# Compressing keys and values inside the projections of a two-block transformer kernel

## The reference, cut to what matters

```python
def compress(kv, pos_emb, w1, w2):
    n_c = (S - CMP_LEN) // CMP_STRIDE + 1                     # 31 blocks of 32 tokens, 16 apart
    blocks = kv[:, blk] + pos_emb[None, None, :, None, :]
    flat = blocks.transpose(0, 1, 3, 2, 4).reshape(B, n_c, G, CMP_LEN * Dh)
    return jax.nn.gelu(flat @ w1) @ w2                        # 2048 -> 128 -> 64
...
k_cmp = compress(kc, pos_k, ck_w1, ck_w2)
v_cmp = compress(vc, pos_v, cv_w1, cv_w2)
s_c = einsum(qc, k_cmp) * scale          # q without rotation
s_s = einsum(qr, k_sel) * scale          # rotated q, rotated keys ks
s_w = einsum(qr, kw_i) * scale           # rotated q, rotated keys kw
```

## Time and profile before

| | before |
|---|---|
| runs (us) | 3473.38, 3473.66, 3468.51; median 3473.38 |
| profiled execution | 3475.57; its span in the trace 3473.8 |
| TensorE busy, share of the span | 3272.7 us, 94% |
| DVE, ACT, POOL busy | 46%, 41%, 46% |
| mean granted TensorE clock | 0.966 |

### The profile page before, as it was taken

How to read it: one execution, slowest core, us unless ns; L and a number is a source line. 1 busy time by engine, 2 the same in 40 slices (tenths; PEclk the granted TensorE clock), 3 DMA queues, 4 the chain that set the end, 5 groups by cost and what they waited for, 6 DMA issues and landing times.

```text
span 3473.8 us, 45512 instructions
## 1 busy us (share of the span) xinstructions
PE 3272.7 (94%) x16902; PEld 2669.8 (77%) x16902; DVE 1596.8 (46%) x2361; ACT 1438.5 (41%) x2575; POOL 1597.1 (46%) x1404
## 2 busy tenths in 40 slices
PE   6789999998999999999988996999999999999998
PEld 4567888876568888788877775888888888888886
DVE  4783443142743431444247875555565562234421
ACT  3355333223764333333235554454454532243332
POOL 4245445652555446444553321444444434464454
PEclk8899999997999999999999997999999999999999
DMA  4111333341013333333332120111111113333332
GB/s 121 45 43 55 97 97 95 94 116 37 1 32 96 96 95 95 91 97 95 96 82 60 51 61 25 31 38 42 38 37 37 41 46 99 98 95 97 97 96 68
DMA packets 471306, 245.86 MB, mean 71 GB/s; under 512 B 13819, under 2 KB 468710, under 8 KB 471014
## 3 DMA queue, kind: packets, MB, share of 16 engines
q1 hardware_dynamic: 470144, 241.33, 24.5%
q10 hardware_dynamic: 998, 2.30, 0.2%
HBM read 241.51 MB, written 2.10 MB: 70 GB/s over the span
## 4 chain that ended last, share of the span: by engine, by line
PE 84%; DVE 9%; ACT 4%; issue 2%; POOL 1%; DMA 0%; ACTq 0%; DVEq 0%; POOLq 0%
PE ps L464 18%; PE ps L466 18%; PE ps L465 18%; PE ps L2207 2%; PE ps L2311 2%; PE ps L2208 2%; PE ps L2209 2%; PE ps L1538 2%; PE ps L2293 2%; PE ps L1548 2%; PE ps L1561 1%; PE ps L1726 1%; PE ps L1799 1%; PE ps L1727 1%; PE ps L1728 1%
## 5 line engine op out<-in xcount | busy, mean ns | idle before, releaser
L446 POOL TENSOR_TENSOR w_lo<-ring,w_hi 128x512 fp32r<-128x512 f32 (+1 forms) x908 | 1222.7, 1368 | 1542.9 <-ACT w_hi L437 1542.9
L437 ACT ACTIVATE w_hi<-ring 128x512 fp32r<-128x512 f32 (+1 forms) x908 | 516.0, 617 | 1269.4 <-PE ps L466 1189.5
L464 PE MATMUL ps<-h_hi,w_hi 128*128 128x512 f32 x1776 | 702.7, 396 | 4.6 <-POOL w_lo L446 4.4
L466 PE MATMUL ps<-h_hi,w_lo 128*128 128x512 f32 x1776 | 693.4, 390 | 0.0
L465 PE MATMUL ps<-h_lo,w_hi 128*128 128x512 f32 x1640 | 640.1, 390 | 0.0
L464 PEld LDWEIGHTS ps<-h_hi,w_hi 128*128 128x128 f32 x1776 | 334.4, 188 | 81.1 <-POOL w_lo L446 6.4
L466 PEld LDWEIGHTS ps<-h_hi,w_lo 128*128 128x128 f32 x1776 | 334.1, 188 | 69.8
L465 PEld LDWEIGHTS ps<-h_lo,w_hi 128*128 128x128 f32 x1640 | 308.8, 188 | 68.2 <-issue 4.8
L465 PE MATMUL ps<-a_lo,w_hi 128*128 128x512 f32 x752 | 292.9, 390 | 0.0
L466 PE MATMUL ps<-a_hi,w_lo 128*128 128x512 f32 x720 | 280.4, 390 | 0.0
L464 PE MATMUL ps<-a_hi,w_hi 128*128 128x512 f32 x720 | 280.4, 389 | 0.0
(11 more groups left out here) (446 smaller groups left out, 5809.7 us busy)
## 6 DMA issues: line engine op xcount, KB each, us to landing
ring<-in_ffn_w_in SPq DMA_DIRECT2D x176, 512.0 KB, 3.8
ring<-in_w_in SPq DMA_DIRECT2D x96, 512.0 KB, 4.0
ring<-in_ffn_w_down SPq DMA_DIRECT2D x32, 512.0 KB, 4.1
ring<-in_ffn_w_out SPq DMA_DIRECT2D x32, 512.0 KB, 3.8
ring<-in_w_o SPq DMA_DIRECT2D x16, 512.0 KB, 4.1
ring<-in_w_branch_gdn SPq DMA_DIRECT2D x16, 512.0 KB, 3.8
ring<-in_nsa_w_in SPq DMA_DIRECT2D x15, 512.0 KB, 3.9
ring<-in_dsa_w_in SPq DMA_DIRECT2D x13, 512.0 KB, 4.1
```

What stands on the lines that cost most here:

```text
L437: act.activation(w_hi[:, (halves(u) + j) % PIECES, 0:n, :], slot(u)[:, j * n:(j + 1) * n, :], ACT.Copy) \
L446: pool.tensor_tensor(w_lo[:, q % PIECES, 0:n, :], slot(u)[:, j * n:(j + 1) * n, :], w_hi[:, q % PIECES, 0:n, :].bitcast(f32), ALU.subtract ...
L464: pe.matmul(dst, wh, hi(k), start=first and k == 0, stop=False)
L466: ins = pe.matmul(dst, wl, hi(k), start=False, stop=last and k == 2 * n - 1)
```

## The change

1. The compression moves into the loop over the projection entries. PE transposes the positions after n=9, ACT copies them at n=10; DVE gathers the blocks of keys at n=12 and of values at n=13; PE makes the first product of keys after n=15 and of values after n=16; ACT takes both GELUs at n=17; PE makes the second products after n=17 and ACT copies them at n=18, ahead of the copy of that entry itself.
2. Both groups stand side by side in one product: 16 products with 62 moving columns for each of keys and values, 32 in all, in place of 64 with 31.
3. The duplicating products (L1388, L1402) go. At n=10 ACT issues four transfers inside SBUF, each of 64 partitions x 4 KB, that write `kv_raw` and `k_rot` with the partition halves exchanged (`kv_swap`, `k_swap`). DVE gathers from `kv_raw` or `kv_swap` in SBUF, where it read PSUM.
4. `k_pad`, its 8 copies and its zeroing go: the scores read `k_rot` or `k_swap` directly, and only one copy of `k_cmp` is written. The factor 1/8 goes into the rotated queries: L1240 and L1242 become scalar_tensor_tensor, with a scale of 1 for the keys and 1/8 for the queries.
5. `pe_attention` waits for the last rotations and copies, `k_swapped` and `nsa_copied` 2.

```diff
-    blk = Area(area.at).take(2, CMP_LEN // 2, NC)
+    blk = [Area(at).take(CMP_LEN // 2, 2 * NC) for at in (area.at, prT_at)]
...
-    k_pad = area.take(2, 2, 2, T)
+    area.take(KT, T)
     gelu_h = area.take(2, 2, 32)
+    swap_area = Area(MEM_AT)
+    kv_swap, k_swap = swap_area.take(2, T), swap_area.take(2, T)
...
-    def pool_key_zeros(pool):
-
-        pool.wait_ge(unit_done.sem, p1["units"][-1] + 1)
-        for b in range(2):
-            pool.memset(k_pad[:, b], 0.0).then_inc(sig("pads_zero").sem, 1)
...
+            if n == N_POS:
+                pe_cmp_positions(pe)
+            elif n in N_HIDDEN:
+                pe_cmp_hidden(pe, N_HIDDEN.index(n))
+            elif n == N_SECOND:
+                pe_cmp_second(pe)
...
+            if n == N_POS + 1:
+                act_cmp_positions(act)
+                act_swap(act, p)
+            elif n == N_SECOND:
+                act_cmp_gelu(act)
+            elif n == N_SECOND + 1:
+                act_cmp_second(act)
...
-            dve.tensor_tensor(e[4], e[3], const("rope_c"), ALU.mult)
+            scale = HD ** -0.5 if done >= 2 else 1.0
+            dve.scalar_tensor_tensor(e[4], e[3], scale, const("rope_c"), ALU.mult, ALU.mult)
             dve.wait_ge(sig("proj_perm").sem, p["perm"] + r + 1)
-            ch.link(dve.tensor_tensor(rt[:, :], ps[:, 4 + r % 2, :], const("rope_s"), ALU.mult))
+            ch.link(dve.scalar_tensor_tensor(rt[:, :], ps[:, 4 + r % 2, :], scale, const("rope_s"), ALU.mult, ALU.mult))
...
+            if n in N_BLOCKS:
+                dve_cmp_blocks(dve, N_BLOCKS.index(n))
...
-    def pe_nsa(pe):
-        pe.wait_ge(sig("proj_rope").sem, p1["rope"] + sum(e[0] == "rope" for e in p1["entries"]))
-        pe.wait_ge(*evac_of(p1, len(p1["entries"]) - 1 - 2 * MEM_PAIRS))
-        pe.wait_ge(*evac_of(p1, len(p1["entries"]) - 1))
-        pe.wait_ge(sig("proj_turned").sem, 3)
-        for b in range(2):
-            for g in range(2):
-                ins = pe.matmul(ps[:, 2 * b + g, :], const(f"dup{g}"), k_rot[:, b, :], start=True, stop=True)
-                ins.then_inc(sig("nsa_dup").sem, 1)
+    N_POS, N_BLOCKS, N_HIDDEN, N_SECOND = MEM_FROM + KT - 1, (12, 13), (15, 16), 17
+
+    def pe_cmp_positions(pe):
         pe.wait_ge(sig("cmp_loaded").sem, 16 * 7)
         for j in range(2):
-            ins = pe.transpose(ps[:, 4, j * CMP_LEN:(j + 1) * CMP_LEN], pos_rows[0:CMP_LEN, j, :],
+            ins = pe.transpose(ps[:, 6, j * CMP_LEN:(j + 1) * CMP_LEN], pos_rows[0:CMP_LEN, j, :],
                                ident[0:CMP_LEN, 0:CMP_LEN])
         ins.then_inc(sig("pos_turned").sem, 1)
+
+    def act_cmp_positions(act):
+        act.wait_ge(sig("pos_turned").sem, 1)
+        act.activation(posT.rearrange("p j l -> p (j l)"), ps[:, 6, 0:2 * CMP_LEN], ACT.Copy).then_inc(sig("pos_ready").sem, 1)
+
+    def act_swap(act, p):
+
+        act.wait_ge(sig("mem_tile").sem, p["mem"] + KT)
+        act.wait_ge(sig("proj_evac").sem, p["evac"] + 3)
+        for e in range(2):
+            act.dma_start(kv_swap[even_odd[e]], kv_raw[even_odd[1 - e]]).then_inc(sig("kv_swapped").sem, 16)
+        act.wait_ge(sig("proj_rope").sem, p["rope"] + 2)
+        for e in range(2):
+            act.dma_start(k_swap[even_odd[e]], k_rot[even_odd[1 - e]]).then_inc(sig("k_swapped").sem, 16)
+
+    def dve_cmp_blocks(dve, j):
+        dve.wait_ge(sig("pos_ready").sem, 1)
+        dve.wait_ge(sig("kv_swapped").sem, 32)
+        dve.wait_ge(sig("proj_turned").sem, 3)
+        for g in range(2):
+            for half in range(2):
+
+                rows_ = even_odd[half]
+                kv = (kv_raw if g == half else kv_swap)[rows_, j, :]
+                src = bass.AP(kv.tensor, kv.offset + half, [kv.ap[0], [2, CMP_LEN // 2], [CMP_STRIDE, NC]])
+                pos = posT[rows_, j, half::2].unsqueeze(2).broadcast_to([HD, CMP_LEN // 2, NC])
+                ins = dve.tensor_tensor(blk[j][rows_, :, g * NC:(g + 1) * NC], src, pos, ALU.add)
+        ins.then_inc(sig("cmp_blocks").sem, 1)
+
+    def pe_cmp_hidden(pe, j):
         pe.wait_ge(sig("w1_loaded").sem, 32)
-        pe.wait_ge(sig("nsa_copied").sem, 4)
+        pe.wait_ge(sig("cmp_blocks").sem, j + 1)
+        for l in range(CMP_LEN // 2):
+            ins = pe.matmul(ps[:, 6 + j, 0:2 * NC], w1[:, j, l, :], blk[j][:, l, :],
+                            start=l == 0, stop=l == CMP_LEN // 2 - 1)
+        ins.then_inc(sig("cmp_hidden").sem, 1)
+
+    def act_cmp_gelu(act):
         for j in range(2):
-
-            if j:
-                pe.wait_ge(sig("cmp_blocks").sem, 2)
-            for g in range(2):
-                ins = pe.matmul(ps[:, 5 + g, :], const(f"dup{g}"), kv_raw[:, j, :], start=True, stop=True)
-                ins.then_inc(sig("cmp_dup").sem, 1)
-            for g in range(2):
-                pe.wait_ge(sig("cmp_blocks").sem, 2 * j + g + 1)
-                for l in range(CMP_LEN // 2):
-                    ins = pe.matmul(ps[:, 2 * j + g, 0:NC], w1[:, j, l, :], blk[:, g, l, :],
-                                    start=l == 0, stop=l == CMP_LEN // 2 - 1)
-                ins.then_inc(sig("cmp_hidden").sem, 1)
-        pe.wait_ge(sig("cmp_gelu").sem, 4)
+            act.wait_ge(sig("cmp_hidden").sem, j + 1)
+            act.activation(gelu_h[:, j, :, 0:NC], ps[:, 6 + j, 0:2 * NC].rearrange("p (g c) -> p g c", g=2),
+                           ACT.Gelu_apprx_tanh).then_inc(sig("cmp_gelu").sem, 1)
+
+    def pe_cmp_second(pe):
+        pe.wait_ge(sig("cmp_gelu").sem, 2)
         for g in range(2):
-            pe.matmul(ps[:, 7, g * 32:g * 32 + NC], w2_k, gelu_h[:, 0, g, 0:NC], start=True, stop=True)
-            ins = pe.matmul(ps[0:NC, 7, 64 + g * HD:64 + (g + 1) * HD], gelu_h[:, 1, g, 0:NC], w2_v, start=True, stop=True)
+            pe.matmul(ps[:, 6, g * 32:g * 32 + NC], w2_k, gelu_h[:, 0, g, 0:NC], start=True, stop=True)
+        for g in range(2):
+            ins = pe.matmul(ps[0:NC, 7, g * HD:(g + 1) * HD], gelu_h[:, 1, g, 0:NC], w2_v, start=True, stop=True)
         ins.then_inc(sig("cmp_done").sem, 1)
 
-    def act_nsa(act):
-        for b in range(2):
-            for g in range(2):
-                act.wait_ge(sig("nsa_dup").sem, 2 * b + g + 1)
-                act.wait_ge(sig("pads_zero").sem, 3 + b)
-                for e in even_odd:
-                    ins = act.activation(k_pad[e, b, g, even_odd.index(e), :], ps[e, 2 * b + g, :], ACT.Copy,
-                                         scale=HD ** -0.5)
-                ins.then_inc(sig("nsa_copied").sem, 1)
-        act.wait_ge(sig("pos_turned").sem, 1)
-        act.activation(posT.rearrange("p j l -> p (j l)"), ps[:, 4, 0:2 * CMP_LEN], ACT.Copy).then_inc(sig("pos_ready").sem, 1)
-        for j in range(2):
-            for g in range(2):
-                act.wait_ge(sig("cmp_hidden").sem, 2 * j + g + 1)
-                act.activation(gelu_h[:, j, g, 0:NC], ps[:, 2 * j + g, 0:NC], ACT.Gelu_apprx_tanh) \
-                   .then_inc(sig("cmp_gelu").sem, 1)
+    def act_cmp_second(act):
         act.wait_ge(sig("cmp_done").sem, 1)
-        for g in range(2):
-            for e in even_odd:
-                ins = act.activation(k_cmp[e, g, even_odd.index(e), 0:NC], ps[e, 7, g * 32:g * 32 + NC], ACT.Copy,
-                                     scale=HD ** -0.5)
-            ins.then_inc(sig("nsa_copied").sem, 1)
+        act.wait_ge(sig("pads_zero").sem, 2)
+        act.activation(k_cmp[:, :, 0, 0:NC], ps[:, 6, 0:64].rearrange("p (g c) -> p g c", g=2)[:, :, 0:NC], ACT.Copy,
+                       scale=HD ** -0.5).then_inc(sig("nsa_copied").sem, 1)
         act.activation(v_cmp[0:NC].rearrange("p (x n) -> p x n", x=5)[:, 1::2, :],
-                       ps[0:NC, 7, 64:64 + 2 * HD].rearrange("p (g d) -> p g d", g=2), ACT.Copy) \
+                       ps[0:NC, 7, 0:2 * HD].rearrange("p (g d) -> p g d", g=2), ACT.Copy) \
            .then_inc(sig("nsa_copied").sem, 1)
-
-    def dve_nsa(dve):
-        dve.wait_ge(sig("pos_ready").sem, 1)
-        for j in range(2):
-            for g in range(2):
-                dve.wait_ge(sig("cmp_dup").sem, 2 * j + g + 1)
-                if j:
-                    dve.wait_ge(sig("cmp_hidden").sem, g + 1)
-                for half in range(2):
-
-                    rows_ = slice(half * HD, (half + 1) * HD)
-                    kv = ps[rows_, 5 + g, :]
-                    src = bass.AP(kv.tensor, kv.offset + half, [kv.ap[0], [2, CMP_LEN // 2], [CMP_STRIDE, NC]])
-                    pos = posT[rows_, j, half::2].unsqueeze(2).broadcast_to([HD, CMP_LEN // 2, NC])
-                    ins = dve.tensor_tensor(blk[rows_, g], src, pos, ALU.add)
-                ins.then_inc(sig("cmp_blocks").sem, 1)
...
-                        u |= dict(q=q_raw[:, pair, tok], k=k_cmp[:, g, hh, 0:NC], bias=cmp_bias[:, t, 0:NC], masked=0,
+                        u |= dict(q=q_raw[:, pair, tok], k=k_cmp[:, g, 0, 0:NC], bias=cmp_bias[:, t, 0:NC], masked=0,
```

(11 more changed lines are left out.)

4 lines of the change are left out of this document (removed).

## The result

| | before | after |
|---|---|---|
| median of 5 runs each (us) | 3473.66 (3468.51 to 3478.0) | 3452.10 (3447.49 to 3455.53) |
| ratio to before | 1 | 0.9938, 95% interval 0.9923 to 0.9952 |
| profiled execution; its span | 3475.57; 3473.8 | 3452.10; 3450.0 |
| mean granted TensorE clock | 0.966 | 0.967 |

The kernel is faster by 21.6 us. The forecast was 29.3 us, or 3444.1; the measured median stands 0.1 us above the top of the range. The sign came out, and so did most of the mechanism; a part of the gain is missing: 7.7 us by the medians, 5.5 us by the spans of the traces (3473.8 and 3450.0).

A forecast was written before the change was run, and what follows sets the result against it. TensorE was taken to bound the kernel, with a serial 41.9 us stage before attention. The terms -41.9 + 2.3 + 6.6 + 0.3 + 3.1 + 1.0 - 0.7 sum to -29.3 us, so 3444.1 us, range 3437 to 3452.

The forecast's parts named there:

- (a): Stage between last projection product and first score goes, -41.9 us; attention's remaining wait for ACT's roundings and copies, +2.3 us.
- (f): Short memk entries before n=17 no longer outrun ACT and POOL, as other products give them time: -0.7 us.
- (b): First products, halved, in PE's own queue: 64 records at 0.103 us, +6.6 us; upper bound 13.4 at 0.209 each.
- (c): Small transposes on PE: +0.3 us; ACT's copy of them at n=10 lies beside PE's next entry.
- (d): GELU at n=17 stands behind ACT's rounding, so PE idles for roundings, table load and GELUs: +3.1 us.
- rival 3: Longer stall at n=17 or n=15, from table-switch drain or gathers blocking with POOL: +1.4 to +4 us, about 3447; chance 0.12.
- (g): DVE's rotations and block gathers, 2.7 to 4.3 us of gathers per entry, finish before PE asks: cost 0.
- (h): ACT's four transfers at n=10, 3.6 us to issue at most, cost nothing; PE is held only from 21 us on.
- Rival 4: Swaps inside SBUF land slowly: costs from 21 us landing time, kernel slower than before from 50 us; chance 0.03.
- (e): Second products, four matmuls of the compression: +1.0 us at full clock (0.8 to 1.9).
- Rival 2: Cold compression: PE drops to half clock inside the moved products, +6.8, +0.9 and +1.7 us, 3453.5 us; chance 0.08.
- rival 1: Warm attention: clock stays at 1.00 over both waits, so attention starts at full clock: 2.8 us less, 3441.3; chance 0.2.

The follow-up runs named there:

- e4: Kernel after, with first and second products, GELU and copies moved behind the last projection entry, gathers and transfers left in place; 3449.24 us, ratio 0.9937.
- e1: Kernel after, but at n=17 ACT takes both GELUs before it rounds unit n+2; 3441.36 us, ratio 0.9908 to the kernel before.
- e2: Kernel after, plus three throwaway products of 512 columns on PE ahead of its wait for GELU at n=17; 3446.41 us, ratio 0.9916.
- e6: Kernel after, idle at n=17 left, plus four throwaway products of 512 columns (eight records) behind the second products; 3457.44 us, ratio 0.9950.
- e5: e1, plus at n=18 ACT copies k_cmp and v_cmp, loads the exponential's table, and copies the entry before rounding; 3444.36 us, ratio 0.9911.
- e9: e5, plus one throwaway product of 512 columns in each of steps 1 to 5 of layer 1's attention; 3437.55 us, ratio 0.9897.
- e3: Kernel after, plus a dummy GELU behind ACT's copy at n=16 that loads the table early; 3444.03 us, ratio 0.9918.
- e8: Kernel before with only the rotated keys' part changed (k_swap, scaled queries, no k_pad), compression left behind the projections; 3469.69 us, ratio 0.9986.
- e7: Kernel after, but first products made per group again, 64 of 31 columns in place of 32 of 62; 3469.54 us, ratio 0.9984.

## Where the prediction was right, and where it failed

**What bounds the kernel: right.** The gain is in the stage: 24.0 us of the stage, 23.8 of the span, with the small differences outside it that are named above.

**(a), (f): right.** The stage is gone, and so is the wait for POOL. What attention waits for is 1.97 us, forecast 2.3, since ACT's two copies are short (0.20 and 0.25 us) and overlap. ScalarE of the kernel after, in order of time:

```profile
816.81 1.15 ACT L439 ACTIVATE w_hi<-ring 128x512 fp32r<-128x512 f32 x2 [11.93 <-PE ps L483]
817.86 0.20 ACT L1455 ACTIVATE square_sum<-ps 128x62 f32<-128x62 f32 x1
817.96 0.25 ACT L1457 ACTIVATE square_sum<-ps 31x128 f32<-31x128 f32 x1
818.12 0.36 ACT L1228 ACTIVATE arena<-ps 128x256 f32<-128x256 f32 x1
```

**(b): right, 7.0 for 6.6 us.** With 62 columns a record still costs about a weight load. The upper bound of 0.209 was real: e4's records took 0.216 at half clock. The Trainium skill (TensorE: Matmul & The Clock Gate, LDWEIGHTS) gives a weight load as its columns divided by 1.2 in ns, 107 ns for 128 columns, and names no clock; the row at full clock agrees (0.110), that of e4 at half clock disagrees, and the measurement decides.

**(c): right**, 0.30 us. **(d): right as an idle**, 2.94 for 3.1 us. ScalarE of the kernel after:

```profile
802.97 1.28 ACT L1441 ACT_TABLE_LOAD   x1
804.26 0.34 ACT L1441 ACTIVATE arena<-ps 128x62 f32<-128x62 f32 x2
```

The roundings end at 802.95, the table load runs from 802.97 to 804.25, and the GELUs start at 804.26. The Trainium skill (ScalarE: Activation LUTs, What ACT_TABLE_LOAD costs) gives a switch a drain of some 1.38 us more; this trace shows 0.02 and 0.01 us around the load, so here it isn't there, and the longer stall of rival 3 falls.

**(g): right in cost, wrong in size.** VectorE of the kernel after, in order of time:

```profile
773.86 2.03 DVE L1427 TENSOR_TENSOR arena<-squares,square_sum 64x496 f32<-64x496 f32 x1
775.90 2.03 DVE L1427 TENSOR_TENSOR arena<-arena,square_sum 64x496 f32<-64x496 f32 x2
...
785.37 1.90 DVE L1427 TENSOR_TENSOR arena<-squares,square_sum 64x496 f32<-64x496 f32 x1
```

The gathers of an entry took 5.1 and 5.0 us, where I had 2.7 to 4.3. Six of the eight took 1.0 us each; two, which began while POOL was in the middle of a split instruction, took 2.03 and 1.90. They were done at 778.97 and 787.27, and PE asked at 786.4 and 792.8, so they cost nothing. Where POOL began a split instruction beside a gather, that one grew in turn: 3.73 us for the unit that starts at 778.05, against 2.58 alone. The Trainium skill (SBUF — State Buffer, Who interferes with whom) says that a DVE instruction with two SBUF inputs contends with a GpSimd instruction that reads SBUF, and that the lock on the shared port is exclusive; the doubled gathers agree. Of the rotations made with scalar_tensor_tensor fifteen took 0.68 or 0.69 us, as the tensor_tensor ones had; one, at 779.61 beside POOL's split, took 1.02.

**(h): right.** DMA issues of the kernel after (KB each, median us from issue to landing):

```profile
arena<-squares ACTq DMA_DIRECT2D x2, 256.0 KB, 3.5
arena<-arena ACTq DMA_DIRECT2D x2, 256.0 KB, 5.4
```

These are medians; the four landed 3.1 to 6.5 us after their issue, against the 21 us from which they would cost something. Rival 4 was far off.

**The clock: here the prediction failed.** The failing step is the sentence that priced the idle at n=17: "entry 18 runs part of its 5.5 us at half speed: up to +1.7 us ... I take neither". Both halves were wrong. The idle did cost the clock, and it cost it for all of entry 18, 5.1 us, and for the second products, 1.5 us in place of 1.0. With +0.4 from (b), and 0.5 less in the two waits, that is 5.5 us, against the 5.3 by which the stage missed. The other 2 us of the 7.7 between the medians are of the size of the differences outside the stage, and no run gives them a cause. e1 and e2 show that the idle was the cause, by opposite means; e6 shows that entry 18 could run at full clock behind the same idle once dense products had won it back.

The bound of 1.7 us is half of 3.3 us, and 3.3 us is the length of the row at 1.00 in the earlier trace rows. The row I should have used is the other one there: 34 records at 0.50 for 7.10 us with PE busy all the time. There narrow products stayed at the lower level to their end, and entry 18 is narrow too. The trace of the kernel before also shows what ended it. Its stretches of the first L1402, of the second, and of L1407 behind the second (the L1407 behind the first is in the earlier trace rows):

```profile
810.50:813.90 3.40, 3.40 (x5) 0.99 (x5) 1.34 (x2) 1.30 (x2) 0.00 (x0) 0.52 0.00 0
824.60:827.60 3.00, 3.00 (x4) 0.93 (x4) 1.12 (x2) 0.20 (x1) 0.00 (x0) 0.50 0.00 0
827.80:831.00 3.20, 3.20 (x29) 3.12 (x29) 1.37 (x3) 0.00 (x0) 0.00 (x0) 1.00 0.00 0
```

Behind PE's idle of 4.4 us the first L1402 ran at half clock; each time four of its records of 512 columns ran at the lower level, the higher one followed, and each time the products of 31 columns then lost it within some 3.3 us. Behind the idle at n=17 the change puts no such dense record. The upper end for a lost clock at n=17 is the whole entry at half clock, 5.5 us more, with the upper end of (e), 0.9 more: 3444.1 + 5.5 + 0.9 = 3450.5 us. This case was in my list of what would make me wrong only through the sum of two waits above 5.4 us; their sum was 4.9, and I was wrong all the same, because what they cost was not their length. Rival 2 stands at 3453.5, close to the 3452.1 measured, but by luck: its largest term, 6.8 us for first products at half clock, did not occur (0.110 a record), and its 1.7 us for n=18 was 5.1.

**Attention cold: right**, pair 0 takes 26.0 us as before. e5 shows that rival 1 would have failed even with nearly no wait ahead of attention: the clock falls 2.1 us after the first score. In e9, with a product of 512 columns in each of five early steps, it did not fall.

**Still open.** Which executions of one kernel keep the clock and which lose it, in the stage (e3, e4, e8) and behind attention (all of them); why all runs of e6 lie so high; and whether the placement of the products is worth anything (e4).

## What to carry to other kernels

Price an idle stretch of TensorE by its length and by what the products behind it cost at half clock, and look in the trace of before for a stream of the same kind that stayed there. Put what TensorE will wait for ahead of what TensorE's own last product releases in the queue of the helping engine: one `if` moved in ACT's loop (e1) took another 8.7 us off the stage and some 10 off the time, by the ratios. Judge an edit worth a few us by the stage in the trace, with a look at the pieces that it doesn't touch: here these differed by up to 13.4 us between executions. Where narrow products share a weight, put them side by side: the count of loads falls, and here (e7 against the kernel after) the clock held as well.

## What the runs showed of the hardware that I had not expected

- At the lower level (1.2 GHz) 56 records of 128 and fewer columns, 11.8 us without a gap, didn't bring the higher one back. In e6 it came back when six records of 512 columns had run, in 5.2 us, and the 48 narrow ones behind them kept it for 5.4 us; in the kernel before it came back twice behind four such records.
- The higher level was lost within an idle time of 2.94 us (kernel after), 0.6 us behind one of 1.66 us (e3, in the traced execution), 2.7 us behind one of 0.90 us (e4), and in e7 with no idle at all, within 64 records of 31 columns. In the kernel before it held over an idle time of 1.77 us with eight records of 512 columns behind it (L1388).
- The same program behind attention took 2451.4 to 2464.8 us, at a granted clock of 0.98 and 0.97.
- Of eight gathers with both inputs in SBUF two took 2.03 and 1.90 us in place of 1.0, those that began during GpSimd's subtraction.
- A transfer of 256 KB from one half of the partitions to the other landed in 3.1 and 3.8 us (the first two issued) and in 4.4 and 6.5 us (the two behind them).
